# Dilated attention with shorter class scores for the first query tile, and layer-norm sums and the pointwise projection of stage three on high and low parts

## The chip, the cores and the metric

The kernel runs on one core of one Trainium2 chip. The metric is device time in microseconds (us), the median over several executions. The chip's engines are named as in the profile: PE (TensorE, matmuls; PEld is its weight loads), DVE (VectorE), ACT (ScalarE), POOL (GpSimd) and SP (SyncE, which issues the transfers of the weights).

## What is computed

One sequence of 256 tokens with 1024 features goes through three blocks, each an attention mixer followed by a gated feed-forward network with a depthwise convolution of width 3. Everything is fp32. The first mixer is a dilated attention, the second a block attention, the third joins an attention with forgetting gates, a conformer convolution and a pooling branch. The two pieces that the change touches are these.

```python
DILATED_PAIRS = ((128, 1), (512, 4), (2048, 16))     # (window, dilation)
# mixer A, for every pair g: query t attends keys t, t-dil, ..., t-window
    scores = jnp.einsum('rnqhd,rnkhd->rnhqk', qr, kc) * ATTN_SCALE
    scores = jnp.where(mask[None, :, None], scores, -jnp.inf)
    m = scores.max(axis=-1); p = jnp.exp(scores - m[..., None]); den = p.sum(axis=-1)
# the three groups are joined by weights den * exp(m - max m)

def layer_norm(x, g, b):
    mu = jnp.mean(xf, axis=-1, keepdims=True)
    var = jnp.mean(jnp.square(xf - mu), axis=-1, keepdims=True)
    y = (xf - mu) * lax.rsqrt(var + EPS)
    return y * g + b

def conformer_conv(u, dw_w, dw_b, ln_g, ln_b, pw_w):
    a, b = jnp.split(u, 2, axis=-1)
    h = a * jax.nn.sigmoid(b)
    h = causal_depthwise_conv(h, dw_w) + dw_b         # width 31
    h = jax.nn.silu(layer_norm(h, ln_g, ln_b))
    return h @ pw_w                                   # 256 x 256
```

## The kernel before

**Streaming weights.** All weights come in chunks from memory (SP issues the transfers) into a ring of six buffers `w_raw`. For each chunk ACT rounds it to the type fp32r (`w_hi`, line 415), DVE subtracts that from the raw weights (`w_lo`, line 423), and PE multiplies high by high, high by low and low by high. So a matmul in fp32r takes three passes over parts where a plain fp32 matmul, which the profile shows as two records, takes one call. ACT splits a chunk four steps ahead of PE, DVE three. An attention chunk is 12 matmuls of 384 columns (lines 708 to 710, inside `unit_chunk_pe`), the output projection uses lines 1357 to 1359, the feed-forward up part lines 455 and 457, its down part lines 1895 to 1897.

**Order.** Every engine has a hand-written program. In the attention stages it is a loop over chunks n, four per head pair (p, o = n // 4, n % 4), and small steps of the mixer stand behind chosen chunks, in the same numbering on PE (`att_c_pe`), ACT (`att_c_act`) and DVE (`att_c_dve`). An engine runs its list strictly in that order, and semaphores join the lists.

**Stage one, mixer A** has eight head pairs. The 256 queries are two tiles qt of 128. Keys of dilations 4 and 16 are sorted in four classes of 64 keys, 32 of each token half. For a pair PE runs `score_a_pe`: `classes(0)` (16 calls of line 888, 32 weight columns, 64 key columns, which the trace shows as 32 records), then the two bands (line 876), then `classes(1)`. DVE masks, ACT takes the exponential, DVE divides. Then `prob_t_a_pe` transposes the probabilities in blocks of 128 (line 905): for qt 0 two blocks per head (classes, band), for qt 1 three. `prob_t_a_act` copies them from PSUM with one activation per qt (line 1103), and `pv_a_pe` multiplies with the values (lines 919, 924, 928). All these use small tiles of the PE array except the transposes; a weight of 64 columns is shown as 128*64.

**Stage three, mixer C** has four head pairs, 16 chunks. Next to the attention it runs the convolution branch: `ln_sum_pe` (line 2185, after chunk 4) and `ln_var_pe` (line 2200, after chunk 5) sum over channels with a 128x128 matrix of ones, both in plain fp32; `ln_rsqrt_act` (lines 2204 and 2207, step 6), `ln_silu_act` (step 7: a table load L2215, two SiLU activations L2218, a table load L2220 back); `pw_pe` (line 2251, after chunk 13) multiplies the 256x256 pointwise weights in plain fp32, four calls, eight records. `decay_pe` (line 825, step 8), `decay_act` (L833) and `decay_dve` (L840) make the forgetting terms that `score_c_pe` (lines 854 and 800, from step 9) needs. For pair 0 the exponentials (`exp_act`, L1126) stand at step 10, the division (`weigh_dve`, L1268 and L1272) at step 11, the transposes (`prob_t_pe`, L943) at step 12, their copy (`prob_t_act`, L1133) at step 12 of ACT, the scores of pair 1 at step 13 of PE.

## Time and profile before

| | us |
|---|---|
| median of 3 runs | 1023.37 (1023.27 to 1023.7) |
| the profiled execution | 1023.5 |
| its span, first to last instruction | 1021.7 |
| PE busy | 1017.2 |
| DVE busy | 879.8 |
| ACT busy | 686.4 |
| granted TensorE clock, share of full speed | 1.000 |

The span is 1.8 us short of the execution's own time, and that execution is 0.13 us above the median. The busy time of an engine counts its instructions; matmuls are pipelined, so the start of one to the start of the next is what it costs, not the length shown.

### The profile page before, as it was taken

Reading aid. Unit: us, or ns where it says so; the run is one execution under the profiler, and the core shown is the slowest. Engines: PE = TensorE matmul, PEld = TensorE weight load, DVE = VectorE, ACT = ScalarE, POOL = GpSimd, SP = SyncE. Lnnn points to the kernel's source line nnn. Section 1 sums busy time; section 2 is a strip of 40 time slices with the busy share of each in tenths; the row PEclk is TensorE's granted clock in tenths of the full one; section 3 lists DMA queues with packets and bytes.
Section 4 is the critical chain, followed back from the end, with each engine's and each line's share of the span. In section 5 each row is a group of like instructions: output and inputs, shape, how many; then the busy total and the mean of one; then the engine's idle time right before and its main releaser. Section 6 shows DMA issues by size and latency. Waiting matters only on the chain.

```text
span 1021.7 us, 22230 instructions
## 1 busy us (share of the span) xinstructions
PE 1017.2 (100%) x8022; PEld 959.0 (94%) x8022; DVE 879.8 (86%) x1535; ACT 686.4 (67%) x1267; POOL 349.8 (34%) x371
## 2 busy tenths in 40 slices
PE   9999999999999999999999999999999999999998
PEld 8999999999999999999999999999998999999998
DVE  7987778787799998887888999988897879999886
ACT  7776666766766665677786766656697777665663
POOL 5412222112256533342111556433340025554332
PEclk9999999999999999999999999999999999999999
DMA  9744465556476666536454566666434537666651
GB/s 319 264 146 152 140 187 157 167 177 195 153 232 200 215 191 198 171 94 215 126 196 150 186 206 210 201 193 196 156 120 140 166 125 215 218 205 196 196 162 42
DMA packets 57753, 183.40 MB, mean 180 GB/s; under 512 B 6352, under 2 KB 9680, under 8 KB 57424
## 3 DMA queue, kind: packets, MB, share of 16 engines
q1 hardware_dynamic: 56816, 181.52, 56.8%
q8 instruction: 45, 0.74, 0.3%
q10 hardware_dynamic: 864, 0.92, 0.3%
q14 instruction: 28, 0.23, 0.1%
HBM read 181.36 MB, written 1.05 MB: 179 GB/s over the span
## 4 chain that ended last, share of the span: by engine, by line
PE 98%; ACT 1%; DVE 0%; DMA 0%; issue 0%; DVEq 0%; ACTq 0%
PE ps L455 23%; PE ps L457 12%; PE ps L708 10%; PE ps L710 9%; PE ps L709 9%; PE ps L1895 6%; PE ps L1897 6%; PE ps L1896 6%; PE ps L1357 2%; PE ps L1359 2%; PE ps L1358 2%; PE ps L634 1%; PE ps L905 1%; PE ps L800 1%; PE ps L943 1%; PE ps L888 1%
## 5 line engine op out<-in xcount | busy, mean ns | idle before, releaser
L423 DVE TENSOR_TENSOR w_lo<-w_raw,w_hi 128x1024 fp32r<-128x1024 f32 (+2 forms) x369 | 440.7, 1212 | 31.8 <-ACT w_hi L415 31.4
L415 ACT ACTIVATE w_hi<-w_raw 128x1024 fp32r<-128x1024 f32 (+2 forms) x369 | 353.2, 972 | 120.1 <-PE ps L457 102.8
L455 PE MATMUL ps<-xg,w_hi 128*128 128x512 f32 x1056 | 362.8, 390 | 0.0
L457 PE MATMUL ps<-xg,w_lo 128*128 128x256 f32 x1056 | 291.5, 276 | 0.0
L455 PEld LDWEIGHTS ps<-xg,w_hi 128*128 128x128 f32 x1056 | 198.2, 188 | 38.9
L2020 POOL TENSOR_TENSOR prob_t<-prob_t,qkT 128x256 f32<-128x256 f32 x63 | 111.0, 1762 | 257.3 <-ACT prob_t L1941 257.3
L457 PEld LDWEIGHTS ps<-xg,w_lo 128*128 128x128 f32 x1056 | 198.2, 188 | 0.1
L708 PE MATMUL ps<-w_hi,xg 128*128 128x384 f32 (+1 forms) x556 | 192.1, 345 | 0.0
L710 PE MATMUL ps<-w_hi,xg 128*128 128x384 f32 (+1 forms) x556 | 187.3, 337 | 0.0
L709 PE MATMUL ps<-w_lo,xg 128*128 128x384 f32 (+1 forms) x556 | 185.7, 334 | 0.0
L1895 PE MATMUL ps<-g_hi,w_hi 128*128 128x256 f32 x528 | 145.9, 276 | 0.0
L1896 PE MATMUL ps<-g_lo,w_hi 128*128 128x256 f32 x528 | 145.8, 276 | 0.0
L1897 PE MATMUL ps<-g_hi,w_lo 128*128 128x256 f32 x528 | 145.8, 276 | 0.0
L2014 POOL TENSOR_TENSOR qkT<-prob,rms_r 128x256 f32<-128x256 f32 x132 | 122.9, 952 | 16.6 <-DVE prob L1955 11.7
L1988 DVE SCALAR_TENSOR_TENSOR qkT<-qkT,par 128x255 f32<-128x255 f32 (+1 forms) x264 | 112.2, 477 | 6.5 <-ACT qkT L1934 6.4
L1934 ACT ACTIVATE qkT<-qkT,par 128x256 f32<-128x256 f32 x132 | 77.9, 598 | 46.0 <-POOL qkT L2014 44.5
L708 PEld LDWEIGHTS ps<-w_hi,xg 128*128 128x128 f32 x556 | 104.2, 188 | 2.1 <-issue 0.7
L710 PEld LDWEIGHTS ps<-w_hi,xg 128*128 128x128 f32 x556 | 104.5, 188 | 0.0
L709 PEld LDWEIGHTS ps<-w_lo,xg 128*128 128x128 f32 x556 | 104.3, 188 | 0.1
L1895 PEld LDWEIGHTS ps<-g_hi,w_hi 128*128 128x128 f32 x528 | 99.1, 188 | 2.5
L1896 PEld LDWEIGHTS ps<-g_lo,w_hi 128*128 128x128 f32 x528 | 99.1, 188 | 0.0
L1897 PEld LDWEIGHTS ps<-g_hi,w_lo 128*128 128x128 f32 x528 | 99.1, 188 | 0.0
(196 smaller groups left out, 1380.1 us busy)
## 6 DMA issues: line engine op xcount, KB each, us to landing
w_raw<-w_stream SPq DMA_DIRECT2D x228, 512.0 KB, 3.9
w_raw<-w_stream SPq DMA_DIRECT2D x137, 384.0 KB, 3.7
w_raw<-w_stream SPq DMA_DIRECT2D x4, 392.0 KB, 3.0
con<-consts SPq DMA_DIRECT2D x1, 1024.0 KB, 7.4
x_all<-x_t SPq DMA_DIRECT2D x4, 256.0 KB, 6.4
conv_taps<-taps SPq DMA_DIRECT2D x1, 1024.0 KB, 7.5
w_raw<-w_stream SPq DMA_DIRECT2D x4, 192.0 KB, 4.4
x_all<-x_a SPq DMA_DIRECT2D x3, 256.0 KB, 5.4
```

Source lines behind the costliest of these rows:

```text
L415: nc.scalar.activation(w_hi[s][:, 0:w], w_raw[s][:, 0:w], ACT.Copy).then_inc(w_hi_done, 1)
L423: nc.vector.tensor_tensor(w_lo(c)[:, 0:w], w_raw[s][:, 0:w], w_hi[s][:, 0:w].bitcast(F32), ALU.subtract).then_inc(w_lo_done, 1)
L455: nc.tensor.matmul(bank(b, 0, 2 * TOK), w_hi[s][:, k * P:(k + 1) * P], xg[:, k, :, :].rearrange("p h t -> p (h t)"), start=(k == 0), stop= ...
L457: last = nc.tensor.matmul(bank(b), w_lo(c)[:, k * P:(k + 1) * P], xg_hi[:, k, :], start=False, stop=(k == KT - 1), skip_group_check=True)
L708: nc.tensor.matmul(out, hi, wh, start=(k == 0), stop=False)
L709: nc.tensor.matmul(out, hi, wl, start=False, stop=False)
L710: last = nc.tensor.matmul(out, lo, wh, start=False, stop=(k == KT - 1))
L1895: nc.tensor.matmul(acc(m), wh, g_hi[b][:], start=first, stop=False, skip_group_check=True)
L1896: nc.tensor.matmul(acc(m), wh, g_lo[b][:], start=False, stop=False, skip_group_check=True)
L1897: last = nc.tensor.matmul(acc(m), wl, g_hi[b][:], start=False, stop=True, skip_group_check=True)
L1988: nc.vector.scalar_tensor_tensor(cv_s[b][s][:, k:TOK], up_s[b][s][:, 0:TOK - k], par_col(f, t, per, i, 4 * s + 2 - k), cv_s[b][s][:, k:TOK ...
L2014: nc.gpsimd.tensor_tensor(up_s[t % 2][s], up_sum[s], rms_r[:], ALU.mult).then_inc(F.up, 1)
```

## The change

There are two parts.

**Stage one.** For query tile 0 only keys of the first token half can be attended, so its class scores are computed over 32 key columns a call (`class_a(qt)` is 64 for tile 0 and 128 for tile 1). The probabilities of tile 0 are 192 wide in place of 256; the mask, exponential and division on it are 64 columns shorter. The class block of tile 0 is now 64 wide: its transpose reads 64 columns and writes 64 partitions, `prob_t_a_act(0)` copies classes and band by two activations, and the unused half of `prob_t` is set to zero once by DVE ahead of the stage.

**Stage three.** The two norm sums and the pointwise projection run in fp32r on parts: `ln_part_act` and `ln_part_dve` split the operand of the sums, `silu_part_act` and `silu_part_dve` that of the projection, `pw_part_act` and `pw_part_dve` the pointwise weights (512 columns, in the feed-forward of stage two at j = 3). `ln_sum_pe` moves from chunk 4 to 5, `ln_var_pe` from 5 to 7, `ln_rsqrt_act` from step 6 to 8, `ln_scale_dve` from 7 to 8, `ln_center_dve` from 5 to 6, `ln_silu_act` from 7 to 9. `conv_mix_act` goes ahead of `mix_act`.

```diff
@@ -135,9 +135,14 @@
+def class_a(qt):
+    return (qt + 1) * CLASS
 def prob_a(qt):
...
-    return (2 + qt) * P
+    return class_a(qt) + (qt + 1) * P
@@ -174,11 +179,10 @@
         for c in range(CLASSES):
-            same = of_class[:, c].reshape(CLASS)
-            keys = (order[:(qt + 1) * P], same, same)
-            parts = [mask(w, d, of_class[qt, c], keys[g]) for g, (w, d) in enumerate(DILATED_PAIRS)]
+            parts = [mask(*DILATED_PAIRS[g], of_class[qt, c], of_class[t, c]) for t in range(qt + 1) for g in range(1, NDIL)]
+            parts.append(mask(*DILATED_PAIRS[0], of_class[qt, c], order[:(qt + 1) * P]))
             o = CON_MASKA + 3 * P * qt
-            con[c * PART:(c + 1) * PART, o:o + prob_a(qt)] = np.concatenate(parts[1:] + parts[:1], axis=1)
+            con[c * PART:(c + 1) * PART, o:o + prob_a(qt)] = np.concatenate(parts, axis=1)
     keys, o = np.concatenate([np.arange(HD * n, HD * n + HD) for n in KEY_BLOCKS]), CON_MASK1
@@ -271,6 +275,10 @@
     fg_hi, fg_lo = [fg_all[:, n, :, :, 0:HEADS_C] for n in range(2)]
+    ones_r = sb("ones_r", [P, P], F32R)
+    ln_hi, ln_lo = mix_hi[:, 2, :], mix_lo[:, 2, :]
+    pw_hi, pw_lo = [m[:, 0:2, :].rearrange("p k t -> p (k t)") for m in (mix_hi, mix_lo)]
+    silu_hi, silu_lo = mix_hi[:, 2:4, :], mix_lo[:, 2:4, :]
     cv_shift = [[cv_s0[:, c * W_SHIFT:(c + 1) * W_SHIFT] for c in range(SHIFTS)],
@@ -389,6 +397,8 @@
     side_lo = sem("side_lo")
+    part_hi, part_lo, PART0 = half_hi, half_lo, HALVES
+    PW_W, LN_SUM, LN_VAR, SILU = 1, 2, 3, 4
     pool_pe = sem("pool_pe")
@@ -873,7 +883,7 @@
                     o = qt * P + c * PART
-                    last = nc.tensor.matmul(bank(SA_BANK + 2 * qt + h, P, (qt + 1) * P)[c * PART:(c + 1) * PART, :],
+                    last = nc.tensor.matmul(bank(SA_BANK + 2 * qt + h, class_a(qt), (qt + 1) * P)[c * PART:(c + 1) * PART, :],
                                             q[lo:hi, o:o + PART], kk[lo:hi, 0:(qt + 1) * P], start=True, stop=True,
@@ -885,9 +895,9 @@
                         o = g * TOK + qt * P + c * PART
-                        last = nc.tensor.matmul(
-                            bank(SA_BANK + 2 * qt + h, (g - 1) * CLASS, CLASS)[c * PART:(c + 1) * PART, :],
-                            q[lo:hi, o:o + PART], keys[lo:hi, :, c, :], start=True, stop=True, skip_group_check=True)
+                        out = bank(SA_BANK + 2 * qt + h, 0, class_a(qt)).rearrange("p (t g l) -> p t g l", g=2, l=PART)
+                        last = nc.tensor.matmul(out[c * PART:(c + 1) * PART, :, g - 1, :], q[lo:hi, o:o + PART],
+                                                keys[lo:hi, 0:qt + 1, c, :], start=True, stop=True, skip_group_check=True)
             return last
@@ -901,8 +911,10 @@
             for n in range(2 + qt):
-                o = (3 * qt + n) * P
-                last = nc.tensor.transpose(bank(SA_BANK + 2 * qt + h, n * P, P), prob[h][:, o:o + P], con[:, CON_ID:CON_ID + P])
+                w = class_a(qt) if n == 0 else P
+                o = 3 * qt * P + (class_a(qt) + (n - 1) * P if n else 0)
+                last = nc.tensor.transpose(bank(SA_BANK + 2 * qt + h, n * P, P)[0:w, :], prob[h][:, o:o + w],
+                                           con[:, CON_ID:CON_ID + P])
         last.then_inc(a.pt, 1)
@@ -1055,7 +1067,7 @@
-        o = (g - 1) * CLASS + t * PART
+        o = t * CLASS + (g - 1) * PART
         return v_class(pr)[o:o + PART]
@@ -1099,10 +1111,12 @@
         past(eng, a.pv, pr, 0, None)
-        w = prob_a(qt)
-        nc.scalar.activation(prob_t[:, :, qt, 0:w],
-                             bank(SA_BANK + 2 * qt, 0, 2 * 512).rearrange("p (h c) -> p h c", c=512)[:, :, 0:w],
-                             ACT.Copy).then_inc(a.ptr, 1)
+        both = bank(SA_BANK + 2 * qt, 0, 2 * 512).rearrange("p (h c) -> p h c", c=512)
+        w = (2 + qt) * P
+        if qt == 0:
+            nc.scalar.activation(prob_t[0:CLASS, :, 0, 0:P], both[0:CLASS, :, 0:P], ACT.Copy)
+        o = P if qt == 0 else 0
+        nc.scalar.activation(prob_t[:, :, qt, o:w], both[:, :, o:w], ACT.Copy).then_inc(a.ptr, 1)
@@ -1677,9 +1691,9 @@
                 conv_pe(eng)
-            if n == 4:
+            if n == 5:
                 ln_sum_pe(eng)
-            if n == 5:
+            if n == 7:
                 ln_var_pe(eng)
@@ -1739,20 +1753,25 @@
                 prob_t_act(eng, 2, p - 3, 0)
+            if n == 5:
+                ln_part_act(eng, LN_SUM)
             if n == 7:
+                ln_part_act(eng, LN_VAR)
                 forget_hi_act(eng)
...
             if n == 6:
-                ln_rsqrt_act(eng)
                 pool_mix_act(eng)
                 forget_log_act(eng)
-            if n == 7:
+            if n == 8:
+                ln_rsqrt_act(eng)
+            if n == 9:
                 ln_silu_act(eng)
+                silu_part_act(eng)
+            if n == N_C - 2:
+                conv_mix_act(eng)
             if o == 2 and p >= 3:
                 mix_act(eng, 2, p - 3)
-            if n == N_C - 2:
-                conv_mix_act(eng)
             if o == 2 and p >= 2:
@@ -1802,7 +1821,13 @@
             if n == 5:
+                ln_part_dve(eng, LN_SUM)
+            if n == 6:
                 ln_center_dve(eng)
+            if n == 7:
+                ln_part_dve(eng, LN_VAR)
+            if n == 10:
+                silu_part_dve(eng)
             if o == 0 and p >= 1:
@@ -1811,7 +1836,7 @@
                 pool_mix_dve(eng)
-            if n == 7:
+            if n == 8:
                 ln_scale_dve(eng)
@@ -1912,6 +1937,8 @@
                 rows_act(eng, 2 * f + 1)
+            if f == 1 and j == 3 and i is None:
+                pw_part_act(eng)
             if not ending:
@@ -1992,6 +2019,8 @@
                 split_lo(eng, c + 2 + AHEAD, cp, i)
+            if f == 1 and j == 3 and i is None:
+                pw_part_dve(eng)
             if last:
@@ -2041,6 +2070,7 @@
                 cols_act(eng, 2)
+                nc.scalar.activation(ones_r[:], con[:, CON_ONES:CON_ONES + P], ACT.Copy)
                 nc.scalar.activation(tri[:], con[:, CON_TRI:CON_TRI + 3 * P], ACT.Copy).then_inc(tri_in, 1)
@@ -2180,9 +2210,45 @@
+    def ln_part_act(eng, no):
+        if no == LN_SUM:
+            eng.wait_ge(conv_acc, 3)
+        else:
+            eng.wait_ge(ln_sq, 3)
+        nc.scalar.activation(ln_hi, cv_e[0], ACT.Copy).then_inc(part_hi, 1)
+    def ln_part_dve(eng, no):
+        eng.wait_ge(part_hi, PART0 + no)
+        nc.vector.tensor_tensor(ln_lo, cv_e[0], ln_hi.bitcast(F32), ALU.subtract).then_inc(part_lo, 1)
+    def ln_rows_pe(eng, no, out):
+        eng.wait_ge(tri_in, 1)
+        eng.wait_ge(part_lo, PART0 + no)
+        nc.tensor.matmul(out, ones_r[:], ln_hi, start=True, stop=False)
+        nc.tensor.matmul(out, ones_r[:], ln_lo, start=False, stop=True).then_inc(ln_pe, 1)
     def ln_sum_pe(eng):
-        eng.wait_ge(conv_acc, 3)
-        nc.tensor.matmul(bank(LN_BANK), con[:, CON_ONES:CON_ONES + P], cv_e[0], start=True, stop=True).then_inc(ln_pe, 1)
+        ln_rows_pe(eng, LN_SUM, bank(LN_BANK))
+    def pw_part_act(eng):
+        nc.scalar.activation(pw_hi, par[:, PAR_PW:PAR_PW + 4 * P], ACT.Copy).then_inc(part_hi, 1)
+    def pw_part_dve(eng):
+        eng.wait_ge(part_hi, PART0 + PW_W)
+        nc.vector.tensor_tensor(pw_lo, par[:, PAR_PW:PAR_PW + 4 * P], pw_hi.bitcast(F32), ALU.subtract).then_inc(part_lo, 1)
+    def silu_part_act(eng):
+        eng.wait_ge(ln_act, 4)
+        for t in range(2):
+            last = nc.scalar.activation(silu_hi[:, t, :], cv_a[t], ACT.Copy)
+        last.then_inc(part_hi, 1)
+    def silu_part_dve(eng):
+        eng.wait_ge(part_hi, PART0 + SILU)
+        for t in range(2):
+            last = nc.vector.tensor_tensor(silu_lo[:, t, :], cv_a[t], silu_hi[:, t, :].bitcast(F32), ALU.subtract)
+        last.then_inc(part_lo, 1)
@@ -2196,8 +2262,7 @@
     def ln_var_pe(eng):
-        eng.wait_ge(ln_sq, 3)
-        nc.tensor.matmul(bank(LN_BANK, TOK), con[:, CON_ONES:CON_ONES + P], cv_e[0], start=True, stop=True).then_inc(ln_pe, 1)
+        ln_rows_pe(eng, LN_VAR, bank(LN_BANK, TOK))
@@ -2244,11 +2309,13 @@
         eng.wait_ge(att[2].qe, 2)
-        eng.wait_ge(ln_act, 4)
+        eng.wait_ge(part_lo, PART0 + SILU)
         for o in range(2):
             for t in range(2):
-                w = PAR_PW + t * 2 * P + o * P
-                last = nc.tensor.matmul(bank(PW_BANK, o * TOK), par[:, w:w + P], cv_a[t], start=(t == 0), stop=(t == 1))
+                w = t * 2 * P + o * P
+                nc.tensor.matmul(bank(PW_BANK, o * TOK), pw_hi[:, w:w + P], silu_hi[:, t, :], start=(t == 0), stop=False)
+                nc.tensor.matmul(bank(PW_BANK, o * TOK), pw_hi[:, w:w + P], silu_lo[:, t, :], start=False, stop=False)
+                last = nc.tensor.matmul(bank(PW_BANK, o * TOK), pw_lo[:, w:w + P], silu_hi[:, t, :], start=False, stop=(t == 1))
         last.then_inc(ln_pe, 1)
@@ -2390,6 +2457,7 @@
             resid_dve_lo(dve, 0, 7)
+            nc.vector.memset(prob_t[CLASS:P, :, 0, 0:P], 0.0)
             gains_dve(dve)
...
             ffn_stage(dve, 0, ffn_dve(0))

```

PE, stage one, pair 0: the transposes of query tile 0, between two streamed matmuls. Before:

```order
L710 MATMUL ps<-w_hi5,xg 128x384
L905 MATMUL ps<-con,prob0 128x128 [waits aA_pn]
L905 MATMUL ps<-con,prob0 128x128
L905 MATMUL ps<-con,prob1 128x128 x2
L708 MATMUL ps<-w_hi0,xg 128x384 [waits w_lo_done]
```

After:

```order
L720 MATMUL ps<-w_hi5,xg 128x384
L916 MATMUL ps<-con,prob0 64x128 [waits aA_pn]
L916 MATMUL ps<-con,prob0 128x128
L916 MATMUL ps<-con,prob1 64x128
L916 MATMUL ps<-con,prob1 128x128
L718 MATMUL ps<-w_hi0,xg 128x384 [waits w_lo_done]
```

Each head's class transpose is now 64 partitions wide in its output and alternates with one of 128.

ACT, stage three, steps 7 to 8: what stands ahead of the copy of the decay rows (L833, from `decay_act`). Before:

```order
L1164 ACTIVATE fg_all<-fg 128x4x8 [waits zeroed,fg_dve]
L2215 ACT_TABLE_LOAD
L2218 ACTIVATE qkT<-qkT,par 128x256 [waits ln_dve] x2
L2220 ACT_TABLE_LOAD
L1118 ACTIVATE qkT<-ps 128x256 [waits aC_qt]
L415 ACTIVATE w_hi<-w_raw 128x768 [waits tiles,w_loaded0]
L1018 ACTIVATE tokbuf<-ps 128x256 [waits aC_ss,aC_unit]
L1018 ACTIVATE tokbuf<-ps 128x256 [waits aC_ss,tiles]
L833 ACTIVATE decay_rows<-ps 40x384 [waits zeroed,decay]
```

After, the same engine in steps 8 to 10, from behind the copies of the decay rows (now line 843) and the values up to the chunk split just ahead of the exponentials of pair 0 (now L1140):

```order
L2269 ACTIVATE ln_x<-ps,con 128x256 [waits ln_pe]
L2272 ACTIVATE ln_x<-ln_x 128x256 [waits ln_act]
L425 ACTIVATE w_hi<-w_raw 128x768 [waits tiles,w_loaded1]
L1041 ACTIVATE ln_q<-ss_q,con,r_c 128x4 [waits aC_ss,aC_nm]
L1041 ACTIVATE ln_q<-ss_q,con,r_c 128x4 [waits aC_ss]
L1044 ACTIVATE r_q<-ln_q 128x8 [waits aC_ln]
L2280 ACT_TABLE_LOAD
L2283 ACTIVATE qkT<-qkT,par 128x256 [waits ln_dve] x2
L2285 ACT_TABLE_LOAD
L2244 ACTIVATE mix_hi<-qkT 128x256 [waits ln_act]
L2244 ACTIVATE mix_hi<-qkT 128x256
L425 ACTIVATE w_hi<-w_raw 128x768 [waits tiles,w_loaded2]
```

The rsqrt pair, both table loads, the SiLU and its two copies now stand between the decay rows and the exponentials of pair 0.

## Rows read from the trace of the kernel before

**Rows 1.** The page: the span, busy time of each engine, the chain that ended last.

```profile
span 1021.7 us, 22230 instructions
...
PE 1017.2 (100%) x8022; PEld 959.0 (94%) x8022; DVE 879.8 (86%) x1535; ACT 686.4 (67%) x1267; POOL 349.8 (34%) x371
...
PE 98%; ACT 1%; DVE 0%; DMA 0%; issue 0%; DVEq 0%; ACTq 0%
```

**Rows 2.** Timeline of PE (start, duration, form): transposes of tile 0 in stage one.

```profile
76.86 0.60 PE L905 MATMUL ps<-con,prob 128*128 128x128 f32 x4
...
77.47 0.34 PE L709 MATMUL ps<-w_lo,xg 128*128 128x384 f32 x1
```

**Rows 3.** Timeline of PE and its weight loads: scores and values of one pair, stage one.

```profile
65.38 0.33 PE L710 MATMUL ps<-w_hi,xg 128*128 128x384 f32 x1
65.64 0.29 PEld L888 LDWEIGHTS ps<-qkT 64*32 64x32 f32 x32 [0.24 <-issue]
65.64 0.45 PE L888 MATMUL ps<-qkT 64*32 64x64 f32 x32
...
67.86 0.64 PE L928 MATMUL ps<-prob_t,v_tok 128*64 128x64 f32 x16
...
68.71 0.34 PE L709 MATMUL ps<-w_lo,xg 128*128 128x384 f32 x1
```

**Rows 4.** Groups of PE by form: count, busy us, mean ns.

```profile
L928 PE MATMUL ps<-prob_t,v_tok 128*64 128x64 f32 x128 | 5.1, 222 | 0.0
```

**Rows 5.** Timeline of PE in stage three: a sum in plain fp32, and the decay.

```profile
776.51 0.59 PE L2185 MATMUL ps<-qkT,con 128*128 128x256 f32 x2
...
777.11 0.34 PE L709 MATMUL ps<-w_lo,xg 128*128 128x384 f32 x1
...
786.93 0.33 PE L710 MATMUL ps<-w_hi,xg 128*128 128x384 f32 x1
787.10 0.65 PE L825 MATMUL ps<-tri,fg_all 128*40 128x384 f32 x6
```

**Rows 6.** Timeline of PE in stage three: the scores of pairs 0 and 1, transposes between.

```profile
789.58 0.33 PE L710 MATMUL ps<-w_hi,xg 128*128 128x384 f32 x1
790.06 0.59 PE L854 MATMUL ps<-decay_rows,head_row 128*128 128x384 f32 x2
...
798.08 0.82 PE L943 MATMUL ps<-con,prob 128*128 128x128 f32 x6
...
800.82 0.51 PE L854 MATMUL ps<-decay_rows,head_row 128*128 128x384 f32 x2
```

**Rows 7.** Timeline of ACT in stage three (start, duration, form, idle before and releaser).

```profile
780.32 0.42 ACT L2207 ACTIVATE ln_x<-ln_x 128x256 f32<-128x256 f32 x1
...
783.61 1.28 ACT L2215 ACT_TABLE_LOAD   x1
784.90 1.09 ACT L2218 ACTIVATE qkT<-qkT,par 128x256 f32<-128x256 f32 x2
...
788.33 0.65 ACT L1018 ACTIVATE tokbuf<-ps 128x256 f32<-128x256 f32 x2
788.86 0.48 ACT L833 ACTIVATE decay_rows<-ps 40x384 fp32r<-40x384 f32 x1
...
794.27 0.40 ACT L1126 ACTIVATE prob<-prob,nmax 128x128 f32<-128x128 f32 x1 [1.51 <-DVE nmax L1263]
...
799.68 0.81 ACT L1133 ACTIVATE prob_t<-ps 128x768 f32<-128x768 f32 x1
```

**Rows 8.** Timeline of DVE in stage three: the second head's division for pair 0.

```profile
796.74 0.55 DVE L1272 TENSOR_SCALAR prob<-prob,rsum 128x128 f32<-128x128 f32 x2
```

**Rows 9.** Timeline of DVE in the feed-forward of stage two.

```profile
588.33 2.35 DVE L423 TENSOR_TENSOR w_lo<-w_raw,w_hi 128x1024 fp32r<-128x1024 f32 x2
...
593.10 0.95 DVE L1977 TENSOR_TENSOR g_lo<-prob_t,g_hi 128x256 fp32r<-128x256 f32 x1
```

**Rows 10.** Timeline of PE there: the first down matmul.

```profile
594.65 0.28 PE L1895 MATMUL ps<-g_hi,w_hi 128*128 128x256 f32 x1
```

## The prediction, made before the changed kernel ran

> **What bounds the kernel now.** I read the page first. PE is busy in 1017.2 of 1021.7 us, and the chain that ended last is PE for 98%, while DVE and ACT have 14% and 33% of idle time [rows 1]. So there is one account to keep: what the change adds to or takes from PE's own stream, and at which places PE would wait for DVE or ACT where it does not today. The second view is PE's timeline, read from start to start and not by the length of a row: a streamed fp32r matmul of 384 columns costs 0.17 us (786.93 to 787.10) [rows 5], and by columns one of 256 costs 0.115. The third is the timeline of ACT and DVE at places where the change puts work ahead of something PE waits for.
>
> **Part one, the transposes of stage one.** Today the four transposes of tile 0 and one streamed matmul take 77.47 - 76.86 = 0.61 us; less 0.17 that is 0.44, or 0.11 for each transpose, and nothing is lost on the way in or out [rows 2]. Both kinds of matmul there use the whole array (128*128). The change makes two of the four 64 weight columns wide. The moving side stays 128 columns (the identity), so none of them gets shorter. What comes in is the switch between widths of array tile, twice in and twice out per pair, since the narrow and the full transposes alternate (narrow, full, narrow, full).
>
> What a switch costs is in the rows of the scores and values. Going in: the matmul ahead of L888 starts at 65.38 and L888 at 65.64, so 0.26 against 0.17, that is 0.09 lost, and the weight load L888 starts only with the matmul, with 0.24 of idle time in front of it, so it is not hidden [rows 3]. That load is of 32 columns; a 64-column one is longer, for which I add 0.03. Coming out: the sixteen narrow matmuls of L928 begin at 67.86 and end at 68.50; at a mean of 222 ns the last began at 68.28 [rows 3, 4]. The second streamed matmul behind them begins at 68.71. Less 0.17 for the first, 0.26 us lie between, where the sixteen follow each other every 0.028 and a lone fp32 transpose takes 0.11. So coming out costs 0.15 to 0.23; I take 0.20. One narrow transpose thus costs 0.12 + 0.20 = 0.32, with 0.24 to 0.38 as bounds that these rows make. Two per pair and eight pairs are sixteen: **+5.1 us** (3.8 to 6.1). Nothing hides it, because PE is the bound.
>
> One row speaks against it: L825 has 40 weight columns and begins 0.17 after the matmul ahead, with no loss on the way in [rows 5]. It is shown as 128*40 and not as 128*64, and what it costs on the way out can't be told from its row. I weigh it as a rival below.
>
> The Trainium skill, TensorEngine Tiling (Array Packing), section Key Properties, says that a change of tiling mode drains the engine. The 0.09 us ahead of L888 agree; by that rule the cost stands, and by the L825 row it does not.
>
> **Part one, the scores.** `classes(0)` keeps its 32 records and halves their columns. In its group the 32 weight loads take 0.29 us, just the time over which the matmuls issue [rows 3]: they are bound by loads and issue, so I take 0. If the time went by columns, half of 0.29 would go per pair, 8 x 0.145 = -1.2. So 0, with -1.2 as the lower end. Mask, exponential and division of tile 0 get 64 columns shorter on DVE and ACT, and `prob_t_a_act(0)` is one activation more; both engines are ahead of PE there (their chunks are split three and four chunks early, and the next pair's value matmuls need the copy), so neither is paid. The one memset on DVE lies ahead of stage one's first split that matters, in DVE's start-up idle time; if that cover were gone it would cost some 0.1 us, once.
>
> **Part two, PE's own stream in stage three.** A sum in plain fp32: L2185 begins at 776.51, the matmul after next at 777.11; less 0.17 that is 0.43 us for its two records, 0.216 each [rows 5]. Two fp32r matmuls of 256 columns are 0.23: -0.20 for `ln_sum`, the same for `ln_var`. The pointwise projection has eight such records, 1.73 us, and becomes twelve fp32r matmuls, 1.38: -0.35. The order has `decay_pe` unchanged at chunk 8, so it comes 0.40 earlier and ends at 787.75 - 0.40 = 787.35 in place of 787.75 [rows 5]. Today the first scores of stage three wait for the decay rows: L854 begins at 790.06, 0.48 after the matmul ahead of it in place of 0.17 [rows 6]. The reason is on ACT: the table loads and the SiLU stand ahead of L833, which starts at 788.86, over 1 us after `decay_pe` [rows 7]. They go behind it, so this wait goes: -0.31. In sum -0.71 up to chunk 9, and -0.35 later.
>
> **Part two, what stands on ACT now.** Between the decay rows and the exponentials of pair 0 come: two rsqrt activations at 0.42, 0.83; two table loads at 1.28, 2.56; the two SiLU, 1.09; their two copies of 256 columns each, 0.65 by L1018, or 0.57 without the overlap of neighbours [rows 7]. That is 5.05 us. Against it stand two credits. L833 begins at about 787.3 in place of 788.86: -1.56. And ACT was idle 1.51 us ahead of the first exponential, waiting for DVE, whose maximum doesn't come later now [rows 7]. So the exponentials start 5.05 - 1.56 - 1.51 = 2.0 us later, at 796.3 in place of 794.3. What is queued behind them: the second head's division (L1272 at 796.74, 0.55 long) and with it the transposes L943 on PE, and further down ACT's list the copy L1133 and with it the scores of pair 1 [rows 6 to 8]. The division ends at about 797.3 + 2.0 less 0.2 (DVE itself is no longer busy with the first head then) = 799.0. PE would reach L943 at 798.08 - 0.71 = 797.4 and starts it at 799.0: 1.6 of wait, +0.95 against today. L1133 ends at 799.68 + 0.81 + 2.0 = 802.5, the scores of pair 1 begin there in place of 800.82: +1.7 against today, so another 0.75 of wait. From there the projection gives 0.35 back. Stage three: 1.7 - 0.35 = **+1.3 us**. Bounds: if the silu and its tables find more idle time than I see (no wait at all), the gains alone stand, -0.7 - 0.35 = -1.05; if every step is 0.4 longer and nothing overlaps, +1.7.
>
> **Part two, the weights of the projection.** `pw_part_dve` subtracts 512 columns in the feed-forward of stage two. Two splits of 1024 columns take 2.35 us, so 512 take 0.59. It stands right ahead of or near `g_lo`, which ends at 593.10 + 0.95 = 594.05 and whose first user on PE starts at 594.65: 0.60 of slack [rows 9, 10]. Cost 0 to 0.5, I take **+0.15**. The copy of the ones and `pw_part_act` on ACT, and the two `ln_part` pairs (a copy and a subtraction of 256 columns), end ahead of their users, `ln_sum` and `ln_var` being moved back by one and two chunks; left where the sums stood, each pair would cost up to 0.42 on ACT (by L2207) and about as much on DVE.
>
> **The sum** against the profiled execution: 1023.5 + 5.1 + 0 + 1.3 + 0.15 = 1030.05. That execution lies 0.13 above the median, so **1029.9**. Of its own ends: lowest 1023.4 + 3.8 - 1.2 + 0.7 + 0 = 1026.7, highest 1023.4 + 6.1 + 1.7 + 0.5 = 1031.7.
>
> **The rivals.**
> - *No cost of a switch.* As the L825 row has it, a narrow weight costs nothing when the rest of the array stays as it is. Then only stage three counts: 1023.4 + 1.3 + 0.15 = 1024.8. For it: the row of 40 columns. Against it: L888 and L928 both show losses at their edges. Chance 0.16.
> - *Half the cost.* The way out overlaps with the next transpose, whose weights (128 columns of probabilities) can be loaded while the narrow one streams: 0.16 each, +2.55: 1023.4 + 2.55 + 1.45 = 1027.4. Chance 0.10.
> - *The narrow transposes also lose their own speed.* A transpose of 128 columns takes 0.11, a plain fp32 matmul two records of 0.108 at 128 columns, so 0.216 [rows 2, 5]. If a narrow tile runs as the second, each of the sixteen costs 0.11 more: +1.7, 1031.6. No narrow transpose is in the rows. The Trainium skill, the same page, section Restrictions, has column tiling and transpose mode excluding each other for fp32 input; by it this rival is what happens, and no row here shows it. Chance 0.12.
> - *Faster.* It has one mechanism and place: columns, not loads, set the pace of `classes(0)` in stage one. Its price is -1.2, and it decides only when no switch costs anything and ACT in stage three is not late: 1023.4 - 1.2 - 1.05 = 1021.1. Chance 0.04, since it needs all three.
>
> **How the numbers follow.** The forecast has 0.58. A measurement here tells about 0.2% from no change, 2.05 us, so "same" is 1021.3 to 1025.4. The case without switches lies in it (0.16), the faster case below it (0.04); forecast, half and slow transposes lie above (0.80). The range goes from the no-switch case, 1024.5, to 1032.8, the third rival with 1.2 for the ends of the other terms; it leaves out the faster case and the outer edges of the rest.
>
> **What would show it.** In stage one: from the first narrow transpose to the second streamed matmul behind, 1.25 us in place of 0.61; 0.61 would mean no switch cost, 0.93 half, 1.47 slow transposes. `classes(0)` to the band, start to start: unchanged, or 0.145 less. In stage three: the first exponential of pair 0 at 2.0 us later against the chunks than before, the transposes of pair 0 beginning with a wait of 1.6 us of PE on DVE's division, the scores of pair 1 with one on ACT's copy, and no wait ahead of the first scores. In the feed-forward of stage two: a short PE wait on `g_lo` at the fourth turn. The prediction is wrong as a whole if the narrow transposes pass at 0.11 us; it is wrong in part two if ACT has its exponentials done before PE gets there.

## The result and the profile after

The changed kernel takes 1024.98 us (median of 22 runs, 1024.54 to 1025.37), the kernel before beside it 1023.39 (22 runs). The ratio is 1.0013, with a 95% interval of 1.0007 to 1.0019. So the change costs between 0.7 and 1.9 us, where I had forecast 6.5. It lies in the range, at its lower end, but in the case that I gave 0.16, and the main term of my sum is not there at all.

The page of the changed kernel, with the span, the busy times and the chain, as in [rows 1]:

```profile
span 1023.2 us, 22260 instructions
...
PE 1016.7 (99%) x8026; PEld 957.7 (94%) x8026; DVE 880.0 (86%) x1541; ACT 690.0 (67%) x1281; POOL 350.1 (34%) x371
...
PE 98%; ACT 1%; DMA 0%; issue 0%; DVE 0%; DVEq 0%; ACTq 0%
```

PE is busy 0.5 us less and the span is 1.5 us longer, so PE now stands still about 2 us more than before. Where, can be read from the starts of its instructions, which the traces give to 0.01 us. Both kernels stream the same 6144 matmuls over weight chunks in the same order. I matched them by number and took the start in the changed kernel minus the start in the kernel before. A stretch in which this difference stays flat is unchanged. From one execution of a kernel to another the difference can move by itself too: in three of the experiments it moves by 0.4 us in a stretch where nothing was changed (see `e11_proj_early`).

| at (us of the kernel before) | changed - before | what lies between |
|---|---|---|
| 50 | -0.17 | start |
| 592 | -0.52 | part one: -0.35 (all of it by 277 us) |
| 600 | -0.21 | feed-forward of stage two, its first turns: +0.31 |
| 774 | -0.19 | nothing |
| 787 | -0.76 | stage three, the norm sums: -0.57 |
| 797 | -0.91 | the first scores: -0.17; up to the transposes of pair 0: +0.02 |
| 800 | +0.81 | those transposes: +1.72 |
| 806 | +1.40 | scores of pair 1 and the projection: +0.59 |
| 860 to the end | +1.45 | nothing more |

The -0.17 at the start is not the change's: in other executions of these kernels that value lies between -0.3 and +0.9.

**Part one.** PE's timeline in the changed kernel at the transposes of tile 0 (start, duration, form), which answers [rows 2], and its weight loads there:

```profile
76.47 0.34 PE L720 MATMUL ps<-w_hi,xg 128*128 128x384 f32 x1
76.64 0.60 PE L916 MATMUL ps<-con,prob 128*64 128x128 f32 x4
77.00 0.42 PE L718 MATMUL ps<-w_hi,xg 128*128 128x384 f32 x1
77.26 0.34 PE L719 MATMUL ps<-w_lo,xg 128*128 128x384 f32 x1
```

```profile
76.30 0.19 PEld L720 LDWEIGHTS ps<-w_hi,xg 128*128 128x128 f32 x1
76.47 0.53 PEld L916 LDWEIGHTS ps<-con,prob 128*64 128x64 f32 x4
```

The group starts 0.17 after the matmul ahead, and from it to the second streamed matmul behind are 77.26 - 76.64 = 0.62 us, against 0.61 before. Over the eight pairs the mean of the two kernels is the same to 0.01 us. I had written 1.25. The second fence has the sign that goes with it: the first narrow weight load begins at 76.47, with the matmul ahead of it, as every hidden load does, and no idle time is noted on it.

PE's timeline at the scores, as in [rows 3]:

```profile
65.20 0.33 PE L720 MATMUL ps<-w_hi,xg 128*128 128x384 f32 x1
65.47 0.35 PE L899 MATMUL ps<-qkT 64*32 64x32 f32 x32
65.70 0.97 PE L886 MATMUL ps<-qkT 64*32 64x128 f32 x32
...
66.92 0.44 PE L931 MATMUL ps<-prob_t,v_tok 128*64 128x128 f32 x4
```

From the last streamed matmul to the value matmuls are 1.72 us in place of 1.76. That is 0.04 for a pair and 0.3 for eight, nearly the whole gain of part one (0.35).

**Part two.** The list of waits (engine, waiting line, releaser: us in total, times, longest) has two entries of PE that the kernel before does not have:

```profile
PE ps L955 <- DVE prob L1286: 1.5, 1, 1.5
...
PE ps L864 <- ACT prob_t L1147: 0.6, 1, 0.6
```

PE's timeline at these two places, which answers [rows 6], and ACT's ahead of them, which answers [rows 7]:

```profile
797.00 0.33 PE L720 MATMUL ps<-w_hi,xg 128*128 128x384 f32 x1
798.83 0.87 PE L955 MATMUL ps<-con,prob 128*128 128x128 f32 x6 [1.50 <-DVE prob L1286]
...
801.46 0.33 PE L720 MATMUL ps<-w_hi,xg 128*128 128x384 f32 x1
802.40 0.62 PE L864 MATMUL ps<-decay_rows,head_row 128*128 128x384 f32 x2 [0.61 <-ACT prob_t L1147]
```

```profile
787.03 0.48 ACT L843 ACTIVATE decay_rows<-ps 40x384 fp32r<-40x384 f32 x1 [0.91 <-PE ps L835]
...
791.06 1.28 ACT L2280 ACT_TABLE_LOAD   x1
792.36 1.10 ACT L2283 ACTIVATE qkT<-qkT,par 128x256 f32<-128x256 f32 x2
793.48 1.28 ACT L2285 ACT_TABLE_LOAD   x1
794.77 0.73 ACT L2244 ACTIVATE mix_hi<-qkT 128x256 fp32r<-128x256 f32 x2
...
796.13 0.39 ACT L1140 ACTIVATE prob<-prob,nmax 128x128 f32<-128x128 f32 x1
...
801.54 0.80 ACT L1147 ACTIVATE prob_t<-ps 128x768 f32<-128x768 f32 x1
```

The exponentials start at 796.13, 1.9 us later than before, and no idle time is left ahead of them. ACT went without a stop from the decay rows through the table loads to them.

The wait ahead of the first scores, which I had forecast to go, is smaller but still there. PE's and ACT's timelines:

```profile
788.82 0.33 PE L720 MATMUL ps<-w_hi,xg 128*128 128x384 f32 x1
789.10 0.62 PE L864 MATMUL ps<-decay_rows,head_row 128*128 128x384 f32 x2
...
788.57 0.47 ACT L2269 ACTIVATE ln_x<-ps,con 128x256 f32<-128x256 f32 x1
```

L864 begins 0.28 us after the matmul ahead, in place of 0.48 before and 0.17 without a wait. The decay rows are no longer what it waits for. `score_c_pe` also waits for the first rsqrt activation (L2269, `ln_act` at 1), the change has put that one behind the decay rows, and it ends at 789.04, 0.06 ahead of L864.

### The profile page after: what moved, and what is told of

Read it like the earlier page. It is cut to its first block, busy times and chain, and to the rows that moved or that the text cites. A ratio compares the mean times of both kernels' runs of the same rounds, so it can differ in the third digit from the quotient of the medians.

```text
span 1023.2 us, 22260 instructions
## 1 busy us (share of the span) xinstructions
PE 1016.7 (99%) x8026; PEld 957.7 (94%) x8026; DVE 880.0 (86%) x1541; ACT 690.0 (67%) x1281; POOL 350.1 (34%) x371
## 3 DMA queue, kind: packets, MB, share of 16 engines
HBM read 181.36 MB, written 1.05 MB: 178 GB/s over the span
## 4 chain that ended last, share of the span: by engine, by line
PE 98%; ACT 1%; DMA 0%; issue 0%; DVE 0%; DVEq 0%; ACTq 0%
PE ps L465 23%; PE ps L467 12%; PE ps L718 9%; PE ps L720 9%; PE ps L719 9%; PE ps L1920 6%; PE ps L1922 6%; PE ps L1921 6%; PE ps L1371 2%; PE ps L1373 2%; PE ps L1372 2%; PE ps L644 1%; PE ps L916 1%; PE ps L810 1%; PE ps L955 1%; PE ps L983 1%
## 5 line engine op out<-in xcount | busy, mean ns | idle before, releaser
L1920 PE MATMUL ps<-g_hi,w_hi 128*128 128x256 f32 x528 | 146.0, 277 | 0.0
L1920 PEld LDWEIGHTS ps<-g_hi,w_hi 128*128 128x128 f32 x528 | 99.1, 188 | 2.6 <-DVE g_lo L2004 0.2
```

The source lines that it names most:

```text
L1920: nc.tensor.matmul(acc(m), wh, g_hi[b][:], start=first, stop=False, skip_group_check=True)
```

## Experiments

The edits are shown against the changed kernel where nothing else is said. The differences of matched starts are always against the one profiled execution of the kernel before.

### Each part alone

`e1_stage1_only` is the kernel before with part one of the diff, `e2_stage3_only` with part two.

> Only part one of the change (shorter class scores, 64-wide class transposes). Theory A (a 64-column weight costs nothing at its edges, the score group gets about 0.03 us shorter a pair): 0.2 to 0.3 us less than before by the matched starts of the streamed matmuls, 1023.1 us, a ratio of 0.9997. Theory B (switches cost what I forecast and something else in the changed kernel hid it): 5 us more, 1028.

Measured: 1023.17 us against 1023.30, ratio 0.9999 (0.999 to 1.0008). The times alone can't tell 0.3 us from nothing. By matched starts part one takes 0.39 - 0.04 = 0.35 us off between 50 and 592 us, the same as in the changed kernel and a little over the 0.2 to 0.3 expected. Theory B is out.

> Only part two (norm sums and projection on parts, all moves in stage three, the split of the pointwise weights in the feed-forward of stage two). Theory A: +0.3 us in that feed-forward and +1.6 us in stage three, 1025.3 us, a ratio of 1.0019. Rival: the two parts interact and this alone is within 0.5 us of before.

Measured: 1025.37 us, ratio 1.002 (1.0011 to 1.0029). As expected. Matched starts: +0.20 in the feed-forward, +1.58 in stage three, 1.78 together. With part one's -0.35 that is 1.43, where the changed kernel has 1.60. So the parts add up to within 0.2 us; 0.11 of the rest lies in the feed-forward (+0.20 against +0.31).

### What an edge belongs to

I had priced the narrow transposes by the losses at the edges of the score and value matmuls. Three kernels ask what those losses belong to, all at the same place, the four transposes of tile 0.

`e6_narrow_rows`:

```diff
-last = nc.tensor.transpose(bank(..., n * P, P)[0:w, :], prob[h][:, o:o + w], con[:, CON_ID:CON_ID + P])
+last = nc.tensor.transpose(bank(..., n * P, w)[0:w, :], prob[h][0:w, o:o + w], con[0:w, CON_ID:CON_ID + w])
```

> The changed kernel with the two narrow transposes cut to 64 rows as well (tile 64*64, the queries above 63 left out of the class part of tile 0). They stream 64 columns, so by columns alone they are 0.05 us shorter each: 0.51 us from the first transpose to the second streamed matmul. Theory A (the edge cost that I read at the scores belongs to a row-narrow tile): 0.1 us on the way into each and up to 0.2 on the way out, 0.7 to 1.1 us. Rival (no edge cost for a transpose at all): 0.5.

Measured (PE and its weight loads):

```profile
77.09 0.33 PE L720 MATMUL ps<-w_hi,xg 128*128 128x384 f32 x1
77.35 0.94 PE L916 MATMUL ps<-con,prob 64*64 64x64 f32 x4
...
78.31 0.33 PE L719 MATMUL ps<-w_lo,xg 128*128 128x384 f32 x1
```

```profile
77.35 0.74 PEld L916 LDWEIGHTS ps<-con,prob 64*64 64x64 f32 x4 [0.24 <-issue]
```

0.96 us where columns alone would give 0.5, and 0.09 more ahead of it. The load starts only with its matmul, and 0.24 of idle time is noted on it: the same mark as at L888 in [rows 3]. So a tile narrow in rows has the edge, for a transpose too, as theory A had it. The one time is 1028.41 us.

`e5_narrow_plain`:

```diff
+if w == CLASS:
+    x = CLASS * h
+    nc.tensor.matmul(bank(SA_BANK + 2 * qt + h, n * P, P)[x:x + w, :], prob[h][:, o:o + w],
+                     con[:, CON_ID:CON_ID + P], start=True, stop=True, skip_group_check=True)
+else:
+    last = nc.tensor.transpose(...)
...
-    nc.scalar.activation(prob_t[0:CLASS, :, 0, 0:P], both[0:CLASS, :, 0:P], ACT.Copy)
+    nc.scalar.activation(prob_t[:, :, 0, 0:P], both[:, :, 0:P], ACT.Copy)
```

> The changed kernel with the two 64-column transposes of tile 0 as plain fp32 matmuls with the identity, the first head's to the lower 64 output partitions, the second head's to the upper 64 (that head's class part of the values is left wrong by it). It asks for speed and for position. Forecast rival (plain fp32 needs twice the time of a transpose): +0.11 us for each, 0.83 us in place of 0.62 from the first transpose to the second streamed matmul. If the edge is paid when the column position changes: some 0.1 to 0.2 more behind the second head's. If a 64-column tile has no edge wherever it lies: nothing more.

Measured (PE, then its weight loads; the one time is 1031.51 us):

```profile
77.18 0.33 PE L720 MATMUL ps<-w_hi,xg 128*128 128x384 f32 x1
77.44 0.43 PE L918 MATMUL ps<-con,prob 128*64 128x128 f32 x2
77.80 0.33 PE L921 MATMUL ps<-con,prob 128*128 128x128 f32 x1
78.06 0.43 PE L918 MATMUL ps<-con,prob 128*64 128x128 f32 x2
78.42 0.33 PE L921 MATMUL ps<-con,prob 128*128 128x128 f32 x1
...
78.77 0.34 PE L719 MATMUL ps<-w_lo,xg 128*128 128x384 f32 x1
```

```profile
77.44 0.19 PEld L918 LDWEIGHTS ps<-con,prob 128*64 128x64 f32 x2 [0.24 <-issue]
77.80 0.14 PEld L921 LDWEIGHTS ps<-con,prob 128*128 128x128 f32 x1 [0.17 <-issue]
```

1.33 us, and 0.09 ahead of it, where I expected 0.83 to 1.0. Both expectations in the text missed. From start to start the narrow ones take 0.36 each (0.216 of it their two records). The full transpose between them takes 0.26 in place of 0.11; the one behind the second takes only 0.06 more than in the changed kernel. The second head, in the upper half of the columns, takes the same 0.36 as the first, so its position adds nothing. Together 0.60 us are lost at the edges of two narrow weights. This is the price that I had forecast, 0.30 for each narrow weight beside its slower form, but only now that the weight is a plain fp32 one. In sum: from 24 to 277 us the matched starts go from -0.17 to 6.10, so against the changed kernel's -0.32 the eight pairs lose 6.6 us, 1.7 of it the slower form (sixteen times 0.11) and 4.9 the edges.

`e7_full_plain` (edit of the kernel before):

```diff
+if qt == 0 and n == 0:
+    nc.tensor.matmul(bank(SA_BANK + h, 0, P), prob[h][:, o:o + P], con[:, CON_ID:CON_ID + P],
+                     start=True, stop=True, skip_group_check=True)
+else:
+    last = nc.tensor.transpose(...)
```

> The kernel before with the two class transposes of tile 0 as plain fp32 matmuls with the identity, still 128 columns wide. It completes the pair with the 64-column plain ones (which took 0.36 us each, and 0.26 for the transpose behind). If the edge belongs to narrow plain fp32 weights alone: 0.11 us more for each and no edge, 0.83 us from the first to the second streamed matmul behind. If any change between plain fp32 and transpose is an edge: 1.2 us or more, as with the narrow ones.

Measured (the one time is 1025.49 us):

```profile
76.88 0.38 PE L906 MATMUL ps<-con,prob 128*128 128x128 f32 x2
77.10 0.27 PE L909 MATMUL ps<-con,prob 128*128 128x128 f32 x1
77.21 0.39 PE L906 MATMUL ps<-con,prob 128*128 128x128 f32 x2
77.44 0.27 PE L909 MATMUL ps<-con,prob 128*128 128x128 f32 x1
...
77.72 0.34 PE L709 MATMUL ps<-w_lo,xg 128*128 128x384 f32 x1
```

0.84 us, the first of the two expectations: 0.11 more for each, and no edge. So going from plain fp32 to transpose is free at full width. Of the forms tried here, a narrow plain fp32 weight and a tile narrow in rows have the edge. A 64-column transpose (this change) has none, though the profile writes 128*64 for it as it does for the plain one, and a 40-column fp32r weight (L825 in [rows 5]) has none on its way in.

### The pointwise weights' split

`e3_pw_split_moved`: `pw_part_act` and `pw_part_dve` stand in stage three (ACT step 5, DVE step 8), with their semaphore counts.

> The changed kernel with only the split of the pointwise weights moved out of the feed-forward of stage two into stage three (ACT step 5, DVE step 8 ahead of the decay). Theory A: the 0.3 us that the streamed matmuls lose at 594 to 598 us is gone, stage three is as in the changed kernel to 0.1 us: 0.3 us less than it. Rival: the loss at 594 us is not this subtraction's and stays.

Measured: the difference is 0.56 at 560, 592, 600 and 700 us, so the loss is gone, and stage three costs 2.15 - 0.59 = 1.56. It is the same in all thirteen traces: the loss of 0.20 to 0.34 at 594 us stands in the five with the subtraction there (changed kernel, e2, e5, e6, e8) and in none of the others. Its one time, 1025.65, is higher than the changed kernel's because this execution was 0.9 us late by 24 us already; one time can't show 0.3 us here, the matched starts can. In the changed kernel DVE's list shows what was in the way:

```profile
588.93 0.68 DVE L2239 TENSOR_TENSOR mix_lo<-par,mix_hi 128x512 fp32r<-128x512 f32 x1
...
593.17 0.95 DVE L2004 TENSOR_TENSOR g_lo<-prob_t,g_hi 128x256 fp32r<-128x256 f32 x1
```

### ACT's list in stage three

`e8_no_silu_tables`:

```diff
-nc.scalar.preload_act_table_set("silu_and_others")
...
-    nc.scalar.activation(cv_a[t], cv_b[t], ACT.Silu, scale=..., bias=...).then_inc(ln_act, 1)
-nc.scalar.preload_act_table_set("natural_log_exp_and_others")
+    nc.scalar.activation(cv_a[t], cv_b[t], ACT.Copy).then_inc(ln_act, 1)
```

> The changed kernel without the SiLU: the two table loads are left out and the two activations are plain copies in the same place (so the convolution branch is left without its norm gain, bias and SiLU). About 2.56 + 0.4 us go from ACT ahead of the exponentials of pair 0. Theory A: those exponentials start up to 1.9 us earlier (then they wait for DVE's maximum), PE's waits of 1.5 and 0.6 us go, stage three ends 2 us earlier against the changed kernel, about 0.9 us under before. Rival (the wait has another cause, such as DVE): they stay.

Measured: 1022.54 us against 1023.47, one run each.

```profile
793.55 0.40 ACT L1140 ACTIVATE prob<-prob,nmax 128x128 f32<-128x128 f32 x1 [0.27 <-DVE nmax L1277]
```

Both waits of PE are gone, and stage three goes from -0.04 to -0.99, that is -0.95 in place of +1.64, 2.6 us less where I expected 2. The gains alone that I had put at -1.05 are real; all the rest of stage three is ACT's time between the decay rows and the exponentials.

`e4_silu_at_7` puts that work back ahead of the decay rows and keeps the sums on parts, the second one after chunk 6. The split of the pointwise weights is moved as in e3. On DVE (not shown) `ln_center_dve` and `ln_part_dve(LN_VAR)` stand right behind `forget_bias_dve`, and `ln_scale_dve` is back at step 7.

```diff
-            if n == 7:
+            if n == 6:
                 ln_var_pe(eng)
...
             if n == 7:
-                ln_part_act(eng, LN_VAR)
+                ln_rsqrt_act(eng)
                 forget_hi_act(eng)
...
                 pool_mix_act(eng)
+                ln_part_act(eng, LN_VAR)
                 forget_log_act(eng)
-            if n == 8:
-                ln_rsqrt_act(eng)
+            if n == 7:
+                ln_silu_act(eng)
             if n == 9:
-                ln_silu_act(eng)
                 silu_part_act(eng)
```

> The changed kernel with the rsqrt and SiLU back at step 7 of ACT, ahead of the decay rows (the square sum on PE at chunk 6, center and parts right behind the first sum on DVE), and the split of the pointwise weights moved into stage three (ACT step 5, DVE step 8). Theory A (the loss is ACT's list between the decay rows and the exponentials): the waits of PE ahead of the transposes of pair 0 (1.5 us) and the scores of pair 1 (0.6 us) go, the 0.3 us at the first scores comes back, and PE's savings stand: 0.5 to 1.2 us under before, 1022.2 to 1022.9 us. Rival (PE is late there for another reason): it stays near 1024.7.

Measured: 1023.80 us against 1023.30, ratio 1.0007 (0.9998 to 1.0016). Better than the changed kernel, but not under before. The two waits went, and another grew:

```profile
PE ps L865 <- DVE decay_rows L851: 1.5, 1, 1.5
```

ACT's list there:

```profile
783.88 0.23 ACT L1179 ACTIVATE fg_all<-fg 128x32 fp32r<-128x32 f32 x1 [1.06 <-DVE fg L1174]
784.13 1.28 ACT L2277 ACT_TABLE_LOAD   x1
...
789.37 0.48 ACT L844 ACTIVATE decay_rows<-ps 40x384 fp32r<-40x384 f32 x1
```

PE comes 0.8 us earlier, but DVE's extra splits delay the gates, ACT waits 1.06 us for them before it loads a table, and the decay rows come 0.5 us later than before (789.37 against 788.86 in [rows 7]). The matched starts say it in numbers: -0.79 by 780, +0.57 at the second sum, +1.30 at the first scores, -0.3 from the projection. What PE saved ahead of 790 was lost at 790. The expectation was wrong: it let the 0.3 us at the first scores come back as they were before. They came back as 1.3 more, because a PE that arrives 0.8 us earlier waits 0.8 us longer there, and the decay rows were 0.5 us later besides.

`e10_table_early` adds to e4 one move: the SiLU table is loaded ahead of `forget_hi_act`, in the idle time. e11 has it too.

```diff
             if n == 7:
                 ln_rsqrt_act(eng)
+                nc.scalar.preload_act_table_set("silu_and_others")
                 forget_hi_act(eng)
...
     def ln_silu_act(eng):
-        nc.scalar.preload_act_table_set("silu_and_others")
```

> The kernel with SiLU back at step 7 (e4) and the SiLU table load put ahead of ACT's wait for the forgetting gates, in which ACT idled for 1.06 us there. Theory (the time at which ACT reaches the decay rows sets stage three, PE's savings ahead of it only turn into waiting): the copy of the decay rows starts 0.8 us earlier (788.5 in place of 789.4), PE's wait ahead of the first scores falls from 1.5 to 0.7 us, and stage three ends 0.8 us earlier than in e4, level with before: 1023.0 us. Rival (that wait is DVE's square sum and scale): less than 0.2 us.

Measured: 1022.90 us against 1023.55, ratio 0.9994 (0.9985 to 1.0003).

```profile
783.61 1.28 ACT L1762 ACT_TABLE_LOAD   x1
784.91 0.23 ACT L1179 ACTIVATE fg_all<-fg 128x32 fp32r<-128x32 f32 x1
...
788.98 0.48 ACT L844 ACTIVATE decay_rows<-ps 40x384 fp32r<-40x384 f32 x1
```

At the first scores +0.15 is lost in place of 1.30, and PE's listed wait there is 0.3 us. Against that execution's start, which by the matched start at 774 us was 0.77 us later than that of e4 (+0.20 against -0.57), the decay rows come 1.16 us earlier, where I expected 0.8. Stage three as a whole is -0.32, against +0.84 in e4 (-0.57 to +0.27). The times say only that it is level with before, as expected.

`e11_proj_early` is the kernel before with part one, the projection alone on parts, both sums as they were, and the early table load; `e12_proj_only` is the same without the early load.

> The kernel before with part one, the projection alone on parts (weights split at ACT step 5 and DVE step 8, SiLU split at steps 9 and 10), both norm sums in plain fp32 where they were, and the SiLU table load ahead of the wait for the forgetting gates. Expected by matched starts: part one -0.3, the wait at the first scores gone -0.3, the projection -0.3, at most 0.3 back at the transposes of pair 0 from DVE's later division: 0.6 to 0.9 us under before, 1022.6 us, a ratio of 0.9993. Rival (the gains end in waits further down): within 0.2 us of the kernel with part one alone.

> As e11 with the table load where it was before. If the early table is what pays, this is 0.3 us slower than e11, lost ahead of the first scores at 790 us (L854 0.48 us behind the matmul ahead of it, as before); if not, the same.

Measured: e11 1022.29 us against 1023.55 beside it, ratio 0.999 (0.9981 to 0.9999), so between 0.1 and 1.9 us under the kernel before, and lower than the changed kernel. I expected 1022.6. e12 had one run, 1022.74. The matched starts from 787 to 793 us go from -0.96 to -1.34 in e11 and stay (-0.54 to -0.55) in e12, so the early load is worth 0.38 there, where I expected 0.3; the projection gives 0.29 and 0.29, part one 0.35 and 0.33. In e11 no wait is left at the three places:

```profile
781.60 1.28 ACT L1759 ACT_TABLE_LOAD   x1
782.89 0.23 ACT L1178 ACTIVATE fg_all<-fg 128x32 fp32r<-128x32 f32 x1
...
786.96 0.48 ACT L843 ACTIVATE decay_rows<-ps 40x384 fp32r<-40x384 f32 x1
...
792.39 0.40 ACT L1140 ACTIVATE prob<-prob,nmax 128x128 f32<-128x128 f32 x1 [0.91 <-DVE nmax L1277]
```

These terms make 0.35 + 0.38 + 0.29 = 1.0 us, and the medians differ by 1.26, which the interval allows. Another 0.4 us of the profiled execution of e11 comes between 742 and 750 us, where the kernels do the same. It stands in those of e1 and e2 too and in none of the others. e12, which differs from e11 in the table load alone, does not have it, so it is not an edit's; what it is stays open.

## Why the prediction failed, point by point

- **What bounds the kernel.** Right: PE's stream and its waits hold the whole difference.
- **The transposes, +5.1.** Wrong, and the step that failed is the transfer of a price from one kind of weight to another. The rows that I took it from are row-narrow tiles (L888) and narrow plain fp32 weights (L928), and their price is real: e5 and e6 show it at this very place. A narrow transpose has no such edge; it measured at most 0.01 for the group of four, so about 0 in place of 5.1. The row that could have told me, L825 with 40 columns, I had seen and given 0.16. There was more in it than I used: a load that the profile shows hidden (no idle noted, started with the matmul ahead) marks a weight without an edge, and the two kinds could have been told apart by that mark. The rule of the Trainium skill that I cited for drains (TensorEngine Tiling (Array Packing), Key Properties) agrees with e5 and e6 (0.60 us lost in e5) and not with the narrow transposes of this change, if those count as another mode. The other rule of the Trainium skill (the same page, Restrictions), that column tiling disables transpose mode for fp32 input, I read as making the transposes slow. They kept 0.11 us each. That fits the reading that a transpose is simply not tiled in columns, so that there is no mode to switch; the runs agree with this but don't prove it.
- **The scores, 0 with -1.2 as the lower end.** The value was 0.3 too high: 0.04 a pair. If columns alone set the pace it would have been 1.2. That loads and issue set it instead fits this and was not tested by itself.
- **PE's savings in stage three, -0.71 to chunk 9.** Measured -0.72 (-0.19 to -0.91), but that the two agree is luck, for both terms were off. The sums gave 0.57 in place of 0.40 (-0.19 to -0.76): with the second sum in plain fp32, PE needed 1.45 us (778.85 to 780.30) for it and the eight 64*64 matmuls behind it, and with the first sum on parts in its place it needs 1.10 (778.22 to 779.32), which is 0.35 and not 0.20. The wait at the first scores gave 0.17 in place of 0.31. I had counted the rsqrt among the work that goes behind the decay rows and not seen that PE waits for its first activation there. The projection gave 0.28 and not 0.35: its twelve matmuls start every 0.12 us.
- **ACT's list.** Right in mechanism and size. Exponentials 796.3 forecast, 796.13 measured; transposes 799.0 and 798.83; scores of pair 1 802.5 and 802.40. This execution ran 0.19 ahead of the kernel before, so by shifts against the chunks the first two are right to 0.02 us and the third came 0.1 later than forecast. Stage three was +1.3 forecast, +1.64 measured. The 0.3 is that 0.1, another 0.1 between L864 and the scores behind it (0.55 in place of 0.44 us at pair 1), and 0.07 less from the projection.
- **The weights' split, +0.15.** Measured 0.31, in the range of 0 to 0.5. It begins where I put it: L1920, the first down matmul, starts at 594.18, 0.05 us after `g_lo` ends. But only 0.05 is lost ahead of it. The second down matmul starts 0.23 us later in place of 0.11, and the 22 behind it follow every 0.119 us in place of 0.113, up to the end of the block at 597 us. Why they go slower behind a short wait is not shown.
- **The sum.** With 0 for the transposes, -0.35 for the scores, +1.64 and +0.31 it is 1.6 us, and the medians differ by 1.59. The rival without a switch cost stood at 1024.8 and is right in its mechanism. That it came to 0.2 us of the time is in part luck: the scores were 0.35 too high, and stage three and the weights 0.5 too low.

## What to carry to other kernels

A price for a mode change of an engine holds for the instruction form it was read from. Before carrying it over, look at whether the weight load next to the new form would be hidden, and at every narrow form that the trace already has, the cheap one first.

In a kernel bound by one engine, microseconds saved ahead of a place where that engine waits are lost there. Find the existing waits (0.3 us behind the usual spacing was enough here), and ask which engine's list sets them. A table load put into that engine's idle time gained 0.38 us (e11 against e12). The reworked norm sums gained nothing in the end: stage three is -0.62 in e11, which leaves them as they were, and -0.32 in e10, which has them.

Where an edit is worth less than the times scatter, match the starts of the same instructions in both traces; that shows 0.05 us and where it is. Check a difference in a second trace with the same edit, for 0.4 us came and went here with none.

## What the runs showed of the hardware

In e5 two plain fp32 weights of 64 columns, each between full-width work, cost 0.60 us beyond their records, 0.30 each, with the first at column 0 and the second at column 64. In e6 two transposes cut to 64*64 cost 0.5 us beyond their columns. In the changed kernel the 64-column transposes cost nothing beyond their 0.11, and in e7 the full-width plain fp32 ones 0.216 and no edge. Halving the columns of a pair's sixteen calls of L899 (tiles of 64*32) saved 0.04 us.

A table load took 1.28 us in every trace, and the activation behind it began at once: 783.61 + 1.28 = 784.89, and the SiLU starts at 784.90 [rows 7].
